# Second attention: from 27 score blocks a head to 15, with two softmax parts joined by their log sums

## The reference

```python
ATT_PATTERNS = ((128, 1), (512, 4), (2048, 16))        # (window, dilation) of three groups
def _dilated_mixer(h, k_sh, v_sh, w_q, w_o, positions):
    q = ... rotary(h @ w_q)                            # 3 groups x 8 heads x 128
    for g, (window, dilation) in enumerate(ATT_PATTERNS):
        o_g, lse_g = _dilated_group_attention(q[:, :, g], k_sh[:, :, g], v_sh[:, :, g], window, dilation)
    wts = softmax(stack(lses), axis=0)                 # weights of the 3 groups, by their log sums
    o = einsum('gbsh,gbshd->bshd', wts, stack(outs))
    return o.reshape(...) @ w_o
```

## Time and profile before

| | |
|---|---|
| median of the runs | 3628.27 us |
| the profiled execution, device time | 3628.96 us |
| its span, first to last instruction | 3627.2 us |
| PE busy over the span | 3350.7 us (92%) |
| DVE, ACT, POOL busy | 1586.7 (44%), 879.7 (24%), 1660.9 us (46%) |
| the second attention, last token copy to first product of w_o | 3020.05 to 3195.07 us |
| mean granted TensorE clock | 0.957 of full |

### The profile page before, as it was taken

One profiled execution on the slowest core, in us unless ns is written; L12 is line 12 of the kernel. 1 busy time (PEld: TensorE's weight loads), 2 busy tenths in 40 slices (PEclk: granted clock), 3 DMA queues, 4 the chain that ended last, 5 costly groups with the idle time before them and its releaser, 6 DMA issues. The chain is left out here.

```text
span 3627.2 us, 43009 instructions
## 1 busy us (share of the span) xinstructions
PE 3350.7 (92%) x16268; PEld 2721.7 (75%) x16268; DVE 1586.7 (44%) x2461; ACT 879.7 (24%) x1563; POOL 1660.9 (46%) x880
## 2 busy tenths in 40 slices
PE   7998889999999798999999977899997997889998
PEld 4888768888998376888778854678886786768887
DVE  5867558703323683110153456434312345653421
ACT  3121231101542462110122244122201113422210
POOL 2540036666884003666546600356664561036664
PEclk9998899999999899999999988899998998999999
DMA  5520026632651101233123300123231221013332
GB/s 213 193 105 1 1 70 238 221 109 83 191 182 47 42 1 58 93 93 110 63 80 97 93 12 1 52 82 98 93 106 64 81 87 43 1 48 97 98 103 71
DMA packets 84841, 319.36 MB, mean 88 GB/s; under 512 B 9232, under 2 KB 11024, under 8 KB 83664
## 3 DMA queue, kind: packets, MB, share of 16 engines
q1 hardware_dynamic: 84688, 317.26, 26.7%
HBM read 315.13 MB, written 2.10 MB: 87 GB/s over the span
## 5 line engine op out<-in xcount | busy, mean ns | idle before, releaser
L318 PE MATMUL two<-h_hi,w_hi 128*128 128x512 f32 x2240 | 884.7, 395 | 25.5 <-POOL w_lo L275 25.5
L320 PE MATMUL two<-h_hi,w_lo 128*128 128x512 f32 x2240 | 881.1, 393 | 0.0
L319 PE MATMUL two<-h_lo,w_hi 128*128 128x512 f32 x2144 | 844.8, 394 | 0.0
L275 POOL TENSOR_TENSOR w_lo<-w_raw,w_hi 128x1024 fp32r<-128x1024 f32 x318 | 779.3, 2452 | 35.0 <-ACT w_hi L338 10.1
L273 POOL TENSOR_SCALAR w_hi<-w_raw 128x1024 fp32r<-128x1024 f32 x298 | 318.1, 1067 | 862.6 <-issue 369.4
L420 POOL TENSOR_SCALAR w_hi<-w_raw 128x1408 fp32r<-128x1408 f32 (+1 forms) x106 | 134.0, 1264 | 861.0 <-PE two L443 587.0
L318 PEld LDWEIGHTS two<-h_hi,w_hi 128*128 128x128 f32 x2240 | 424.0, 189 | 120.8 <-issue 17.9
L320 PEld LDWEIGHTS two<-h_hi,w_lo 128*128 128x128 f32 x2240 | 424.3, 189 | 94.2
L319 PEld LDWEIGHTS two<-h_lo,w_hi 128*128 128x128 f32 x2144 | 406.4, 190 | 87.7
L422 POOL TENSOR_TENSOR w_lo<-w_raw,w_hi 128x1408 fp32r<-128x1408 f32 (+1 forms) x112 | 340.1, 3038 | 10.5 <-ACT w_hi L478 1.6
L443 PE MATMUL two<-hid_hi,w_lo 128*128 128x512 f32 x704 | 275.9, 392 | 0.0
(11 more groups left out here) (419 smaller groups left out, 5479.7 us busy)
## 6 DMA issues: line engine op xcount, KB each, us to landing
w_raw<-w_f0u SPq DMA_DIRECT2D x88, 512.0 KB, 3.5
row_raw<-ada SPq DMA_DIRECT2D x48, 512.0 KB, 5.3
w_raw<-w_ssm SPq DMA_DIRECT2D x48, 512.0 KB, 3.5
w_raw<-w_f0d SPq DMA_DIRECT2D x32, 704.0 KB, 4.1
w_raw<-w_f1u SPq DMA_DIRECT2D x44, 512.0 KB, 3.5
w_raw<-w_f2u SPq DMA_DIRECT2D x44, 512.0 KB, 3.5
w_raw<-w_f3u SPq DMA_DIRECT2D x44, 512.0 KB, 3.5
ada_raw<-ada SPq DMA_DIRECT2D x32, 512.0 KB, 3.7
```

The lines of the kernel that those rows point to most:

```text
L275: nc.gpsimd.tensor_tensor(s_lo[s][:, 0:self.kt], w_raw[j][:, 0:self.kt], s_hi[s][:, 0:self.kt].bitcast(f32), ALU.subtract).then_inc(split_ ...
L318: nc.tensor.matmul(dst, s_hi[s][:, k], hi, start=kk == 0, stop=False)
L319: nc.tensor.matmul(dst, s_hi[s][:, k], lo, start=False, stop=False)
L320: last = nc.tensor.matmul(dst, s_lo[s][:, k], hi, start=False, stop=kk == self.parts * self.kt - 1)
```

## The change

- The queries, keys and values of the two dilated groups are stored in token classes: token 4i+r goes to column 128r+i. The ACT copy that empties PSUM (L1726 before) does it by its access pattern, for 8 of the 12 tiles of `kv` and 16 of the 24 of `q2`. Tokens of one class modulo 4 then form a contiguous block of 128, and a query of dilation 4 or 16 needs only the keys of its own class block.
- A head becomes two units instead of four: an even "near" unit (dilation 1: 4 query blocks, each against its own and the preceding key block, 7 blocks in use) and an odd "far" unit (dilations 4 and 16: 4 class blocks, each against the one key block of either group, 8 blocks). 15 blocks a head in place of 27.
- The masks are added by PE: a product of the identity with the mask (`ident_r` x `band_r` or `mask2_r`, fp32r, 512 columns, two a unit) opens each bank before the scores add to it. DVE takes the maximum straight from PSUM, and ACT the exponentials straight from PSUM, 256 columns at a time (4 instructions a unit, each with its row sum).
- Near and far are two softmaxes. They are joined by w = 1/(1+exp(d)), d the difference of their log sums: PE spreads the two log sums over the partitions (`spread`, 8 products of 128 columns; the four of the far unit are written to PSUM with a step of 4 columns, to undo the classes), DVE bounds d at 40, ACT forms exp, ln(1+.), exp(-.) and DVE mixes: far - w*(far - near). The far result is copied out of PSUM by ACT back into token order.
- SP loads the masks earlier (after the input of `Gemm(w_q)` is ready, not after `Tokens`), in two loads of 512 and 128 KB for three of 128, 256 and 256 KB. ACT loads a table and rounds the masks to fp32r before the first scores.

The whole attention has 120 transposes and 120 value products, before 216 and 216.

```diff
-                    nc.scalar.copy(self.dst[:, bass.ds(4 * i + n, 1)].rearrange("p o t -> p (o t)"), g.out(n)).then_inc(mm_free, 1)
+                    dst, src = self.dst[:, 4 * i + n], g.out(n)
+                    if 4 * i + n in self.classes:
+                        dst, src = dst.rearrange("p (r i) -> p i r", r=4), src.rearrange("p (i r) -> p i r", r=4)
+                    nc.scalar.copy(dst, src).then_inc(mm_free, 1)
...
+            def blocks(self, u):
+                return [(n, e) for n in range(4) for e in range(2) if u % 2 or n or e]
+            def col(self, u, what):
+                return d_col[:, u % 4, ("max", "neg", "sum", "inv", "ln", "lse").index(what)]
+            def sp(self, sp):
+                sp.wait_ge(*self.early)
+                for name, dst in (("band", d_band), ("dilated", d_mask)):
+                    a, w = CST[name]
+                    sp.dma_start(dst[:], cst[:, a:a + w]).then_inc(phase_in, 16)
+            def pe(self, pe):
+                def scores(u):
+                    h, dst = u // 2, two[u % 2]
+                    if u >= 2:
+                        pe.wait_ge(*upto(self.p_exp, u - 1))
+                    for b in range(2):
+                        m = mask2_r[:].unsqueeze(1).to_broadcast([P, 2, 256]) if u % 2 else band_r[:, 512 * b:512 * b + 512]
+                        nc.tensor.matmul(dst[:, 512 * b:512 * b + 512], ident_r[:], m, start=True, stop=False)
+                        for n in (2 * b, 2 * b + 1):
+                            for e in range(2 if u % 2 else 1):
+                                if u % 2:
+                                    q, k, w = q2[:, 8 * (e + 1) + h], kv[:, 2 * (e + 1) + h // 4, n * P:(n + 1) * P], P
+                                elif n:
+                                    q, k, w = q2[:, h], kv[:, h // 4, (n - 1) * P:(n + 1) * P], 256
+                                else:
+                                    q, k, w = q2[:, h], kv[:, h // 4, 0:P].unsqueeze(1).to_broadcast([P, 2, P]), 256
+                                last = nc.tensor.matmul(dst[:, 256 * n + P * e:256 * n + P * e + w], q[:, n * P:(n + 1) * P], k, start=False,
+                                                        stop=n % 2 == 1 and P * e + w == 256)
+                    last.then_inc(self.qk[0], 1)
+                def turned(u):
+                    pe.wait_ge(*upto(self.p_normed, u + 1))
+                    blocks = self.blocks(u)
+                    for g in range(2):
+                        if u >= 1:
+                            pe.wait_ge(*upto(self.pt_copied, 2 * u + g - 1))
+                        for j, (n, e) in enumerate(blocks[4 * g:4 * g + 4]):
+                            last = nc.tensor.transpose(ps[4 + g][:, j * P:(j + 1) * P], d_p[u % 4][:, 256 * n + P * e:256 * n + P * e + P], ident[:])
+                        last.then_inc(self.pt[0], 1)
+                def values(u):
+                    h, dst = u // 2, ps[6 + u % 2]
+                    if u >= 2:
+                        pe.wait_ge(*(upto(self.bounded, h) if u % 2 else upto(self.diff, 2 * h - 1)))
+                    blocks = self.blocks(u)
+                    for j, (n, e) in enumerate(blocks):
+                        if j % 4 == 0:
+                            pe.wait_ge(*upto(self.pt_copied, 2 * u + j // 4 + 1))
+                        v = v2[:, (2 * (e + 1) + h // 4) * 4 + n] if u % 2 else v2[:, h // 4 * 4 + n - 1 + e]
+                        last = nc.tensor.matmul(dst[:, n * P:(n + 1) * P], v, d_pt[u % 2][:, j], start=e == 0 or (n, 0) not in blocks, stop=e == 1)
+                    last.then_inc(self.pv[0], 1)
+                def spread(h):
+                    pe.wait_ge(*upto(self.lse, 2 * h + 2))
+                    pe.wait_ge(*upto(self.far, h + 1))
+                    for n in range(4):
+                        nc.tensor.matmul(ps[7][:, n * P:(n + 1) * P], self.col(2 * h, "lse")[:, n:n + 1].to_broadcast([P, P]), ident[:], start=n == 0, stop=False)
+                    for c in range(4):
+                        last = nc.tensor.matmul(ps[7][:, :].rearrange("p (i r) -> p r i", r=4)[:, c], self.col(2 * h + 1, "lse")[:, c:c + 1].to_broadcast([P, P]),
+                                                ident[:], start=False, stop=c == 3)
+                    last.then_inc(self.rows[0], 1)
+                pe.wait_ge(*self.gate)
+                pe.wait_ge(*upto(self.masks, 2))
+                for u in range(16 + 3):
+                    if 0 <= u - 2 < 16:
+                        turned(u - 2)
+                    if u % 2 == 0 and u >= 4:
+                        spread((u - 4) // 2)
+                    if u < 16:
+                        scores(u)
+                    if 0 <= u - 2 < 16:
+                        values(u - 2)
+            def dve(self, dve):
+                for u in range(16 + 5):
+                    if u < 16:
+                        dve.wait_ge(*upto(self.qk, u + 1))
+                        if u >= 4:
+                            dve.wait_ge(*upto(self.p_ln, u - 3))
+                            if u % 2 == 0:
+                                dve.wait_ge(*upto(self.rows, u // 2 - 1))
+                        sig(nc.vector, nc.vector.tensor_reduce(self.col(u, "max"), two[u % 2][:, :].rearrange("p (n k) -> p n k", n=4), AX.X, ALU.max), self.row_max)
+                        sig(nc.vector, nc.vector.tensor_scalar(self.col(u, "neg"), self.col(u, "max"), -SCALE, None, ALU.mult), self.neg_max)
+                    h = (u - 4) // 2
+                    if u % 2 == 0 and 0 <= h < 8:
+                        dve.wait_ge(*upto(self.far, h + 1))
+                        if h >= 2:
+                            dve.wait_ge(*upto(self.hi, h - 1))
+                        sig(nc.vector, nc.vector.tensor_tensor(d_out[h % 2][:], d_far[h % 2][:], ps[6][:], ALU.subtract), self.diff)
+                    if 0 <= u - 1 < 16:
+                        m = u - 1
+                        dve.wait_ge(*upto(self.p_exp, m + 1))
+                        sig(nc.vector, nc.vector.reciprocal(self.col(m, "inv"), self.col(m, "sum")), self.p_inv)
+                        p = d_p[m % 4][:, :].rearrange("p (n k) -> p n k", n=4)
+                        nc.vector.tensor_tensor(p, p, self.col(m, "inv").unsqueeze(2).to_broadcast([P, 4, 256]), ALU.mult).then_inc(self.p_normed[0], 1)
+                        dve.wait_ge(*upto(self.p_ln, m + 1))
+                        a, b = ("ln", "neg") if m % 2 else ("neg", "ln")
+                        nc.vector.tensor_tensor(self.col(m, "lse"), self.col(m, a), self.col(m, b), ALU.subtract).then_inc(self.lse[0], 1)
+                    if u % 2 == 0 and 0 <= h < 8:
+                        dve.wait_ge(*upto(self.rows, h + 1))
+                        if h >= 1:
+                            dve.wait_ge(*upto(self.diff, 2 * h))
+                        nc.vector.tensor_scalar(d_w[:], ps[7][:], 40.0, None, ALU.min).then_inc(self.bounded[0], 1)
+                    h = (u - 5) // 2
+                    if u % 2 == 1 and 0 <= h < 8:
+                        dve.wait_ge(*upto(self.weight, h + 1))
+                        dve.wait_ge(*upto(self.diff, 2 * h + 1))
+                        sig(nc.vector, nc.vector.tensor_tensor(d_out[h % 2][:], d_out[h % 2][:], d_w[:], ALU.mult), self.diff)
+                        nc.vector.tensor_tensor(d_out[h % 2][:], d_far[h % 2][:], d_out[h % 2][:], ALU.subtract).then_inc(self.mixed[0], 1)
+                        dve.wait_ge(*upto(self.hi, h + 1))
+                        nc.vector.tensor_tensor(o2_lo[h][:], d_out[h % 2][:], o2_hi[h][:].bitcast(f32), ALU.subtract).then_inc(self.lo[0], 1)
+            def act(self, act):
+                nc.scalar.preload_act_table_set(LN_EXP)
+                act.wait_ge(phase_in, self.val)
+                nc.scalar.copy(band_r[:], d_band[:]).then_inc(self.masks[0], 1)
+                nc.scalar.copy(mask2_r[:], d_mask[:]).then_inc(self.masks[0], 1)
+                act.wait_ge(*self.gate)
+                for u in range(16 + 5):
+                    if 0 <= u - 2 < 16:
+                        m = u - 2
+                        if m >= 2:
+                            act.wait_ge(*upto(self.pv, m - 1))
+                        for g in range(2):
+                            e = 4 if m % 2 or g == 0 else 3
+                            act.wait_ge(*upto(self.pt, 2 * m + g + 1))
+                            nc.scalar.copy(d_pt[m % 2][:, 4 * g:4 * g + e], ps[4 + g][:, 0:e * P].rearrange("p (j t) -> p j t", j=e)).then_inc(self.pt_copied[0], 1)
+                    h = (u - 5) // 2
+                    if u % 2 == 1 and 0 <= h < 8:
+                        act.wait_ge(*upto(self.bounded, h + 1))
+                        astep(nc.scalar.activation(d_w[:], d_w[:], ACT.Exp))
+                        astep(nc.scalar.activation(d_w[:], d_w[:], ACT.Ln, bias=ones[:, 0:1]))
+                        nc.scalar.activation(d_w[:], d_w[:], ACT.Exp, scale=-1.0).then_inc(self.weight[0], 1)
```

(31 more changed lines are left out.)

54 lines of the change are left out of this document (33 added, 21 removed).

## The result

| | before | after |
|---|---|---|
| time, median of 7 runs each, us | 3630.26 (3615.33 to 3634.08) | 3604.3 (3602.09 to 3607.73) |
| ratio, 95% interval | | 0.9939 [0.9923, 0.9954] |
| time and span of the profiled execution, us | 3628.96, 3627.2 | 3604.3, 3602.5 |
| mean granted clock | 0.957 | 0.959 |
| token copies' end to the first product of w_o, us | 175.02 | 145.44 (forecast 148.4) |

The kernel is 0.61% faster, 26 us, and the forecast of 3604 holds. The profiled spans differ by 24.7: 29.6 less in the attention, 3.6 more in w_o, and 0.65 and 0.6 more ahead and behind.

What follows compares the result with a forecast made beforehand. The prediction took the head's loop of waits between engines as the bound, no engine being full. Attention -175.0 + 148.4, w_o +2.3 and class copies +0.4 gave -23.9: 3605.1, stated as 3604; forecast range 3597 to 3611, eight in ten 3591 to 3620.

Steps and rivals of the forecast that it cites:

- 7.4 + 8.9: One changed head at the high clock: first half from the near maximum 7.4 us, second half 8.9, together 16.3.
- the second half: From the far maximum: maximum, bound, exponentials, logarithm, far copy, `spread`, next near scores and four hand-overs, summed to 8.9 us.
- the far copy: ACT's copy of the far result out of PSUM, behind exponentials and logarithm, with `spread` waiting for it: 0.59 us.
- stepped writes cost twice: Rival: `spread`'s four stepped products and the far copy take 1.6 us more a head, 13 in all: 3617; chance 0.10.
- the cover named for them: PE's 5.5 us of products a tile hide 22 of 24 changed class copies; the other two cost 0.2 us each.
- head 0: First head, without difference or `spread` and partly at the low clock: 10.5 us.
- First maximum: Start of the attention: table load, mask roundings and near scores at the low clock put the first maximum at 7.2 us.
- a fall in one head of three to two: PE's waits lower the granted clock in that share of heads, 0.7 us a head on average, making 17.0 us.
- +2.3: w_o begins at the low clock after PE has nothing to do for 6 us: 2.3 us lost, up to 2.7.
- The four-times rival: Stepped writes of `spread` and the far copy cost four times, with more clock falls: 52 us more, 3656; chance 0.05.
- two falls a head (3615): Rival: the clock falls in both halves of every head, at most 22 us more, put at 11; chance 0.20.
- none (3594): Rival: the clock never falls in the steady heads, and nothing is lost at w_o; chance 0.15.

Runs made afterwards that it cites:

- The doubled products: Kernel after with the four opening value products of every near unit made twice, 3602.56 us; in a second run those of every far unit, 3599.99 us.
- the moved `spread`: Kernel after with `spread` behind the next near scores in PE's order and its columns kept for eight units, not four; 3579.6 us, ratio 0.9865.
- The kernel with idle products: Kernel after plus 20 unused identity products on PE behind the last `spread`, ahead of w_o; 3597.51 us, ratio 0.9925.
- the one with w_o by head: Kernel after with the products of w_o waiting for each head's result instead of for all heads; 3595.08 us, ratio 0.9912.
- the last kernel: Kernel after with `spread` behind the scores, w_o waiting by head, near value products behind the far scores, difference behind the normalisation; 3573.86 us, ratio 0.9844.
- loops of 15.15 and 15.70: Kernel after with the far copy ahead of its unit's exponentials on ACT, 3590.31 us; and with the far copy written straight, 3597.85 us.
- the seven kernels with the idle end: Kernel after and six experiments in which PE stands idle for 6 us ahead of w_o; w_o took 45.65 to 47.91 us.

## Why the prediction was right

**The bound: right.** Not the work of an engine but the loop over PE, DVE and ACT set the head. The doubled products, 0.89 or 0.00 by place, and the moved `spread` show it. Twelve of 27 blocks take off a fifth, 20.5 to 16.2, but I had compared a head with a fall to one without: at one clock the loop is about a seventh shorter, the rest is the clock.

**One head: right, with sizes off that cancelled.** Predicted 7.4 + 8.9 at the high clock, measured 7.19 + 8.98. The terms written down for the second half add up to 9.1 and not 8.9; the slip left the forecast 0.2 a head too short. Of its terms the far copy was put at 0.59 and took 1.06, +0.47; the exponentials at 4 x 0.61 = 2.4 and took 1.94, -0.46. An exponential of 256 columns takes 0.47 and the next starts 0.45 behind its start: the read of the accumulator lies wholly beside them, where I had let 0.09 of its 0.19 overlap. The far copy's error is the rival "stepped writes cost twice", true for ACT (1.8 to 1.9 times) and false for PE. Of its 13 us, 8 x 0.47, less than 4, were there. The class copies were wrong by the same factor, but the cover named for them held.

**The start and the end: right but for head 0.** First maximum 7.44 (7.2), head 0 8.88 (10.5), head 1 15.30 (15.6), from head 7's near maximum to w_o 29.79 (30.1). Head 0 is the largest miss, 1.6 us: it was priced at one and a half times the high clock's durations, but the granted clock was back at 1.00 before its transposes (3033.82).

**The clock: the mean right, its cause only in part.** I had a fall in one head of three to two, 0.7 us each; two of five fell, and heads 2 to 6 took 84.0 for 85. The kernel with idle products and the one with w_o by head have the same heads, and there the same two fell. I had expected a fall from the length of the wait. One loop fits: at 13.36 us a head PE waits 1.2 us at most and no head falls. The rest does not: a wait of 3.06 us in head 0 of the kernel after (ahead of 3033.82) had no fall and one of 3.00 in the last kernel had one, after the same wait of 2.24 us the clock fell in one head and not in the next, one fall came behind a wait of 0.80, three of five heads fell in loops of 15.15 and 15.70, none with 0.9 us more near work, two with 0.9 us more far work. A fall costs a head of the changed kernel 1.5 to 1.6 us, close to the 1.7 of the earlier trace rows. What decides which head falls stays open.

**w_o: right mechanism, the size a matter of the execution.** +2.3 was taken, under a bound of 2.7 from 5.5 us of low clock at the start of w_kv. In the profiled execution w_o ran about 6 us at the low clock and +3.6 came, over the bound; the idle products took back 3.4. Over the seven kernels with the idle end it was +1.3 to +3.6, on average +2.2.

**The sum.** 145.4 for 148.4 and +3.6 for +2.3, with 1.2 us of drift elsewhere: -24.7 in the span for -23.9. The median agrees to 0.3 us, closer than its parts allow: with a stretch ahead that moves by up to 9 us either way, that is luck. It was also reckoned from 3628.27, the median of three runs; the seven runs of the kernel before gave 3630.26, so the gain was 26.0 for a forecast of 24.3. The four-times rival fell with the 0.89 of L1996 and the 1.06 of the far copy. The rivals on the clock, two falls a head (3615) and none (3594), both fell with the two heads of five.

## What to carry to other kernels

- Where engines hand work round in a loop, write out the loop of one turn with its waits before you count blocks or busy time. What shortens it is work out of the loop's path, often by one place in an engine's order: here the late `spread` gave 22 us in the attention, where taking 12 of 27 blocks away had given 30.
- Price each access pattern from a row of its own, and name the cover of each cost put at little: the class copies were mispriced as much as the far copy, but only the copy on the loop counted.
- Compare loops at the same granted clock. A turn with a fall in it against one without shows a gain that is in part the clock's: here about 1.6 of 4.3 us a head.
- When a stretch ahead varies more than the effect, compare stage with stage in the traces; let the next big product start on the parts that are ready, so that PE neither stands idle nor begins at the low clock.

## What was new of the hardware

- An ACT copy from PSUM to SBUF of 512 fp32 columns takes 0.57 to 0.59 written straight, 1.06 with a step of 4 elements and 1.09 with 128. A PE write to PSUM with a step of 4 columns costs nothing for fp32 products of 128 columns.
- In a loop with the same 2.24 us wait of PE in each turn of 16 to 17 us the clock fell in two turns of five, in none with 0.9 us more near work (the attention then cost 1.5 us more in all), and in two again with 0.9 us more far work. The cause is not shown.
- w_o of 193 product records takes 44.3 us begun at the high clock and 45.7 to 47.9 begun at the low one, by how much of the low stretch lay ahead of it.
